# A hybrid attention, HGRN2 and MLP block: the means of query and key squares as two rounded passes, with GpSimd making remainders, and a reordered first stage

## The reference

```
u = rmsnorm(x);  proj = u @ w_in            # 1024 x 4096: q, k, v of attention, hq, two gates, hv, hg
y_na = neighbourhood attention, 8 heads of 64:
       q, k = rmsnorm over the 64 of each head (mean of squares, then rsqrt), times a weight
       scores on a window of 8 rows by 16 columns of a 16 x 64 grid, plus bias; softmax; times v
y_hg = HGRN2, 4 heads of 128, forward and backward, normed and gated
h = x + concat(y_na, y_hg) @ w_out
h = h + relu(rmsnorm(h) @ w_up)^2 @ w_down  # 4096 hidden
```

## Time and profile before

| | us |
|---|---|
| median of 3 runs | 1322.95 |
| profiled execution | 1322.97 |
| its span | 1321.0 |
| PE busy | 1289.5 (98%) |
| DVE busy | 868.1 (66%) |
| ACT busy | 583.6 (44%) |
| POOL busy | 478.3 (36%) |
| mean granted clock of PE | 0.996 |

### The profile page before, as it was taken

One profiled execution on the slowest core, in us unless ns is written; L12 is line 12 of the kernel. 1 busy time (PEld: TensorE's weight loads), 2 busy tenths in 40 slices (PEclk: granted clock), 3 DMA queues, 4 the chain that ended last, 5 costly groups with the idle time before them and its releaser, 6 DMA issues.

```text
span 1321.0 us, 17673 instructions
## 1 busy us (share of the span) xinstructions
PE 1289.5 (98%) x6432; PEld 1079.9 (82%) x6432; DVE 868.1 (66%) x1260; ACT 583.6 (44%) x1049; POOL 478.3 (36%) x259
## 2 busy tenths in 40 slices
PE   7999899999999999999999999999999999999998
PEld 5767787998888888887887788888888788888887
DVE  3456567551788795977468655455455898888885
ACT  5436566444344453333145645445544333432341
POOL 3251121123323132123423545545443454445452
PEclk9999899999999999999999999999999999999999
DMA  8341333232111011023420654444469563443433
GB/s 257 110 129 32 76 97 92 63 95 64 33 32 29 21 32 33 17 97 150 137 96 5 211 167 144 143 152 161 131 218 325 198 237 109 141 162 112 146 95 142
DMA packets 134324, 154.92 MB, mean 117 GB/s; under 512 B 11360, under 2 KB 89440, under 8 KB 134240
## 3 DMA queue, kind: packets, MB, share of 16 engines
q1 hardware_dynamic: 130032, 147.04, 34.6%
q10 hardware_dynamic: 4208, 6.76, 1.4%
HBM read 109.72 MB, written 44.04 MB: 116 GB/s over the span
## 4 chain that ended last, share of the span: by engine, by line
PE 84%; DVE 8%; ACT 3%; issue 2%; DMA 1%; POOL 1%; SPq 0%; ACTq 0%; DVEq 0%
PE bank L2288 8%; PE bank L2292 8%; PE bank L2291 8%; PE bank L2257 7%; PE bank L2260 7%; PE bank L2261 7%; PE bank L2003 5%; PE bank L2007 5%; PE bank L2006 5%; PE bank L2087 3%; PE bank L2214 2%; PE bank L2218 2%; PE bank L2217 2%; PE bank L1901 1%; PE bank L1990 1%
## 5 line engine op out<-in xcount | busy, mean ns | idle before, releaser
L927 POOL TENSOR_TENSOR a_split<-a_raw,a_split 128x1024 fp32r<-128x1024 f32 x56 | 148.0, 2658 | 166.1 <-ACT a_split L1200 166.1
L2257 PE MATMUL bank<-set,w_hi 128*128 128x512 f32 x448 | 177.8, 397 | 1.4 <-issue 1.1
L2260 PE MATMUL bank<-set,w_hi 128*128 128x512 f32 x448 | 176.2, 393 | 0.0
L2261 PE MATMUL bank<-set,w_lo 128*128 128x512 f32 x448 | 176.0, 393 | 0.0
L2288 PE MATMUL bank<-w_hi,a_split 128*128 128x512 f32 x448 | 174.6, 390 | 0.2
L2292 PE MATMUL bank<-w_hi,a_split 128*128 128x512 f32 x448 | 174.3, 389 | 0.0
L2291 PE MATMUL bank<-w_lo,a_split 128*128 128x512 f32 x448 | 174.3, 389 | 0.0
L2003 PE MATMUL bank<-uT_hi,w_hi 128*128 128x512 f32 x384 | 160.8, 419 | 2.5 <-DVE h_gate L1445 2.1
L2007 PE MATMUL bank<-uT_hi,w_lo 128*128 128x512 f32 x384 | 150.9, 393 | 0.0
L2006 PE MATMUL bank<-uT_lo,w_hi 128*128 128x512 f32 x384 | 150.3, 391 | 0.0
L874 POOL TENSOR_TENSOR w_hi<-stage,one_col 128x1024 fp32r<-128x1024 f32 x16 | 30.4, 1902 | 228.1 <-DVE bias L1489 95.9
(11 more groups left out here) (225 smaller groups left out, 2822.1 us busy)
## 6 DMA issues: line engine op xcount, KB each, us to landing
a_raw<-a_dram SPq DMA_DIRECT2D x56, 512.0 KB, 3.7
a_dram<-abuf SPq DMA_DIRECT2D x111, 256.0 KB, 2.1
stage<-in_w_in SPq DMA_DIRECT2D x29, 512.0 KB, 4.2
raw<-in_w_down SPq DMA_DIRECT2D x10, 1024.0 KB, 8.1
stage<-in_w_up SPq DMA_DIRECT2D x16, 512.0 KB, 5.2
raw_b<-in_w_up SPq DMA_DIRECT2D x16, 512.0 KB, 5.7
x_tok<-in_x SPq DMA_DIRECT2D x8, 512.0 KB, 9.9
v_dram<-vs ACTq DMA_DIRECT2D x16, 256.0 KB, 2.5
```

Source lines behind the costliest of these rows:

```text
L927: pool.tensor_tensor(split_of(m, 1), a_raw[:, m % 4, :, :], split_of(m, 0).bitcast(F32), ALU.subtract).then_inc(b_lo, 1)
L2257: first = pe.matmul(dst, w[0], u[0], start=k == 0 and p in (1, 5, 6, 7), stop=False, skip_group_check=True)
L2260: pe.matmul(dst, w[0], u[1], start=False, stop=False, skip_group_check=True)
L2261: ins = pe.matmul(dst, w[1], u[0], start=False, stop=k == 3, skip_group_check=True)
```

## The change

- The means: ACT, behind the square, writes a rounded copy of the squares into `sq_split` (which lies over the value store `vs`, so that the first copy waits for value stores); POOL subtracts it from the squares into the second half (`square_lo`); PE makes two passes of rounded matmuls with a rounded copy of the constant matrix (`mean_r`) instead of one full float32 matmul. `qk_average(n - 1)` comes after four k steps of unit n instead of two, for n = 9 to 12. In the steps its place is as before.
- The low squares stand in POOL's list between splits: squares 0 and 1 ahead of the split of tile 8, 2 and 3 ahead of 9, 4 and 5 ahead of 10, and so on, two by two. The splits of tiles 8 and 9 wait in addition for the low parts of units 9 and 11. The loop over later splits is written out, and the splits of tiles 22 to 24, 25 to 27 and 29 to 31 wait for the end of the levels of head 0, 1 and 2; tile 32 waits, as 33 did, for the last head's.
- First stage: SP loads the identity alone ahead of the second token tile, and that ahead of the first value weights; the norm weights go on SP's queue behind them, the rest of the tables behind the tokens. ACT and DVE normalise a pair of tokens ahead of the value units of the pair before. The arithmetic for the gates' bounds and the clearing of `q_tiles` are moved ahead of the last value units.
- Band 2 is loaded ahead of tile 13 instead of 14. The first `hv` unit is in step 9 instead of 10, and ACT takes it at the end of that step.
- In the MLP's start POOL waits for three of DVE's sums ahead of its fifth low part, and ACT takes set 8 ahead of the first result.

The diff, cut to its core:

```
-VALUE_UNITS = {10: (0, 1, 2), 11: (3, 4, 5), ...
-BANDS_BEFORE = {14: (2, 3, 4), 15: (5, 6), ...
+VALUE_UNITS = {9: (0,), 10: (1, 2), 11: (3, 4, 5), ...
+BANDS_BEFORE = {13: (2,), 14: (3, 4), 15: (5, 6), ...
...
             load_x(0)
+            sp.dma_start(ident, tables[:, 0:P]).then_inc(tab_load, 16)
+            load_x(1)
             load_v_weights(0)
-            sp.dma_start(tab[:, :], tables).then_inc(tab_load, 16)
-            load_x(1)
+            ... sp.dma_start(norm_w[:, 0, :], ...).then_inc(norm_load, 16)
...
+            def square_lo(i):
+                pool.wait_ge(qk_sq_hi, i + 1)
+                pool.tensor_tensor(sq_split[:, 1, :], qk_t[:, 0, :], sq_split[:, 0, :].bitcast(F32), ALU.subtract).then_inc(qk_sq_lo, 1)
+            squares = 0
             for n in range(RING, 4 * RING):
+                if n in (8, 9):
+                    upto = 2 * (n - 7)
+                else:
+                    upto = min(max(2 * n - 14, 0), 16)
+                while squares < upto:
+                    square_lo(squares)
+                    squares += 1
+                if n in (8, 9):
+                    pool.wait_ge(qk_ready, qk_count(FIRST_QK + 2 * (n - 8) + 1))
                 if 10 <= n < 16:
                     pool.wait_ge(bias_done, bias_ops(2 * n - 19))
                 split_one(n)
-            split_turns(4, N_IN // RING)
-            for n in range(N_IN, N_IN + RING):
-                if n == N_IN + 1:
+            for n in range(4 * RING, N_IN + RING):
+                if 22 <= n < 28:
+                    pool.wait_ge(lev_taken, HEAD_PARTS * ((n - 16) // HG_GROUP - 1))
+                elif 29 <= n < N_IN:
+                    pool.wait_ge(lev_taken, HEAD_PARTS * (HG_HEADS - 1))
+                elif n >= N_IN:
                     pool.wait_ge(lev_taken, HEAD_PARTS * HG_HEADS)
                 split_one(n)
...
-            pool.wait_ge(t13_sum, 8)
+            pool.wait_ge(t2_sum, 3)
             up_lo(4)
...
                 act.activation(qk_t[:, 0, :], bank[n % 2][:, :], ACT.Square).then_inc(qk_sq, 1)
+                act.wait_ge(qk_sq, n - FIRST_QK + 1)
+                if n == FIRST_QK:
+                    act.wait_ge(v_stored[0], 32 * 4)
+                act.activation(sq_split[:, 0, :], qk_t[:, 0, :], ACT.Copy).then_inc(qk_sq_hi, 1)
...
-                pe.wait_ge(qk_sq, n - FIRST_QK + 1)
+                pe.wait_ge(qk_sq_lo, n - FIRST_QK + 1)
...
-                pe.matmul(bank[7][:, :], head_mean, qk_t[:, 0, :], start=True, stop=True).then_inc(qk_mean, 1)
+                pe.matmul(bank[7][:, :], mean_r[:, :], sq_split[:, 0, :], start=True, stop=False)
+                pe.matmul(bank[7][:, :], mean_r[:, :], sq_split[:, 1, :], start=False, stop=True).then_inc(qk_mean, 1)
...
-                projection(n, range(2))
+                projection(n, range(4))
                 qk_average(n - 1)
-                projection(n, range(2, KT))
+                projection(n, range(4, KT))
```

More of the change, by code:

```diff
@@ L50 @@
 FBLK = 2
+HG_GROUP = 3
 OUT_BLOCKS = KT // FBLK
@@ L151 @@
 STEP_UNIT = {s: BEFORE + 1 + s for s in range(-2, 9)}
[L153 to L155 removed]
+VALUE_UNITS = {9: (0,), 10: (1, 2), 11: (3, 4, 5), 12: (6, 7, 8), 13: (9, 10, 11), 14: (12, 13), 15: (14, 15)}
+BANDS_BEFORE = {13: (2,), 14: (3, 4), 15: (5, 6), 16: (7, 8), 17: (9, 10, 11), 18: (12, 13, 14), 19: (15,)}
 FIRST_HEAD = list(range(UNIT[("ff", 0, 0)], UNIT[("hq", 0, 1)] + 1))
@@ L237, in hybrid_block @@
         vs = nc.alloc_sbuf_tensor_at("vs", [P, 2, 2, HALF], F32, offset=end_attention)
+        sq_split = nc.alloc_sbuf_tensor_at("sq_split", [P, 2, HALF], F32R, offset=end_attention)
+        mean_r = nc.alloc_sbuf_tensor_at("mean_r", [P, P], F32R, offset=end_attention + 8192)
         x_tok = nc.alloc_sbuf_tensor_at("x_tok", [P, TT, D], F32, offset=work)
@@ L421, in hybrid_block @@
         tab_load = sem("tab_load")
+        mean_load = sem("mean_load")
         norm_load = sem("norm_load")
@@ L443, in hybrid_block @@
         qk_sq = sem("qk_sq")
+        qk_sq_hi = sem("qk_sq_hi")
+        qk_sq_lo = sem("qk_sq_lo")
+        mean_ready = sem("mean_ready")
         qk_mean = sem("qk_mean")
@@ L684, in _ @@
             load_x(0)
+            sp.dma_start(ident, tables[:, 0:P]).then_inc(tab_load, 16)
+            load_x(1)
             load_v_weights(0)
-            sp.dma_start(tab[:, :], tables).then_inc(tab_load, 16)
-            load_x(1)
+            with nc.allow_non_contiguous_dma(reason="small parameter vector"):
+                sp.dma_start(norm_w[:, 0, :], attn_norm_w.rearrange("o (k p) -> p (o k)", p=P)).then_inc(norm_load, 16)
             load_v_weights(1)
@@ L695, in _ @@
                 load_x(t)
+            sp.dma_start(tab[:, P:3 * P], tables[:, P:3 * P]).then_inc(mean_load, 16)
             for n, (kind, where) in enumerate(TILES):
@@ L840, in _ @@
         def _(pool):
[L841 to L850, removed]
             pool.wait_ge(ready_cols, 2)
@@ L861, in _ @@
                 pool.tensor_tensor(v_weight(w_lo, k), v_raw_weight(k), hi.bitcast(F32), ALU.subtract).then_inc(w_split, 1)
[L863 to L868, removed]
             def split_one(n):
@@ L1203, in _ @@
             act.preload_act_table_set("natural_log_exp_and_others")
-            with nc.allow_non_contiguous_dma(reason="small parameter vector"):
-                act.dma_start(norm_w[:, 0, :], attn_norm_w.rearrange("o (k p) -> p (o k)", p=P)).then_inc(norm_load, 16)
             act.wait_ge(ready_cols, 2)
@@ L1218, in _, with rms_pair @@
             v_weights(7)
-            for g in range(1, T_PAIRS):
+            def rms_pair(g):
                 for t in (2 * g, 2 * g + 1):
@@ L1222, in _ @@
                     rms(0, t)
+            rms_pair(1)
+            for g in range(1, T_PAIRS):
                 for k in range(KT):
                     take_uT(g, k)
+                if g + 1 < T_PAIRS:
+                    rms_pair(g + 1)
                 unit(2 * g - 2)
                 unit(2 * g - 1)
+                if g == 2:
+                    act.wait_ge(lb_diff, 1)
+                    act.activation(lb[:, :, :], lb[:, :, :], ACT.Exp).then_inc(lb_exp, 1)
             for dst, a, b in ((na_mask[:, :, :, :].rearrange("p s r c -> p (s r c)"), M_NA, M_END),
@@ L1229, in _ @@
                 act.dma_start(dst.bitcast(I32), masks[:, a // 4:b // 4]).then_inc(mask_load, 16)
+            act.wait_ge(mean_load, 16)
+            act.activation(mean_r[:, :], head_mean, ACT.Copy).then_inc(mean_ready, 1)
             unit(TT - 2)
             unit(TT - 1)
-            act.wait_ge(lb_diff, 1)
-            act.activation(lb[:, :, :], lb[:, :, :], ACT.Exp).then_inc(lb_exp, 1)
             for n in range(FIRST_QK, BEFORE - 2):
@@ L1246, in _ @@
                 values = [UNIT[("hv", 0, 0)] + i for i in VALUE_UNITS.get(s, ())]
-                for n in values[:1]:
+                for n in values[:1] if s > 9 else ():
                     unit(n)
@@ L1250, in _ @@
                     take_pT(s, 2)
-                for n in values[1:2]:
+                for n in values[1:2] if s > 9 else ():
                     unit(n)
@@ L1266, in _ @@
                         score_exp(s + 2, g)
+                if s == 9:
+                    for n in values:
+                        unit(n)
                 if s >= 0:
@@ L1317, in _ @@
             up_weights(5)
+            take_set(8)
             take_c11(0)
-            for g in range(8, 16):
+            for g in range(9, 16):
                 take_set(g)
@@ L1622, in _ @@
             dve.memset(one_col[:, :], 1.0).then_inc(ready_cols, 1)
[L1623 to L1626, removed]
+            for t in range(4):
+                normalise_tokens(0, t)
+                if t == 1:
                     dve.wait_ge(norm_load, 16)
+                    for k in range(KT):
+                        take_uT(0, k)
+            for g in range(1, T_PAIRS):
                 for k in range(KT):
                     take_uT(g, k)
-                if g:
-                    value_lo(2 * g - 2)
-                    value_lo(2 * g - 1)
-            dve.wait_ge(uT_done, 16)
[L1634 to L1641, removed]
+                if g + 1 < T_PAIRS:
+                    normalise_tokens(0, 2 * g + 2)
+                    normalise_tokens(0, 2 * g + 3)
+                value_lo(2 * g - 2)
+                value_lo(2 * g - 1)
+                if g == 1:
+                    dve.wait_ge(c_load, CONSTS)
+                    dve.tensor_tensor(lb[:, :, :], lb_raw[:, :, 1, :], lb_raw[:, :, 0, :], ALU.subtract).then_inc(lb_diff, 1)
+            dve.wait_ge(uT_done, 16)
+            for i in range(2):
+                dve.memset(q_tiles[:, i, :, :, :, :].bitcast(F32), 0.0).then_inc(cleared, 1)
             dve.wait_ge(lb_exp, 1)
@@ L1648, in _ @@
             dve.wait_ge(params, 1)
+            value_lo(TT - 2)
+            value_lo(TT - 1)
+            dve.wait_ge(mask_load, 32)
             for n in range(FIRST_QK, BEFORE - 2):
```

(8 more changed lines are left out.)

2 lines of the change are left out of this document (1 added, 1 removed).

## The result

The changed kernel took 1324.48 us (median of 20 runs, 1321.89 to 1331.16), the kernel before 1322.13 in 20 runs on the same chips: ratio 1.0022 [1.0011, 1.0032], so slower by about 3 us. The forecast was 8.1 us slower: the sign was right and the time lay in the range, the size was wrong. The profiled execution took 1331.16 us with a span of 1329.3, more than any other of the 20: that it equals the forecast is chance. A second profile of the same kernel (experiment 1) took 1325.47 and stands nearer to the median.

What follows compares the result with a forecast made beforehand. TensorE, busy 1289.5 of 1321.0 us, was taken as the bound. Terms of -2.7, +20.4, +1.7, -6.8, -3.0 and -1.5 sum to +8.1 on 1322.95, so 1331 us, range 1316 to 1338.

Steps and rivals of the forecast that it cites:

- the clock behind the stands: TensorE's clock drops after its three stands before means 8, 10 and 12: 7.0 us lost (1.7, 2.8, 2.5).
- Later, -1.5: After step 9: gathered splits free VectorE, 0.5 us off h_gate waits; 1.0 us gained in the MLP's start.
- first stage: Kernel start: earlier token tile 1 (1.3 us) and no x_tok waits in third transposes (1.4 us), together 2.7 us gained.
- order on GpSimd: Means 8 to 14: low squares queue behind splits, so TensorE stands; 20.4 us lost, 13.4 queueing and 7.0 clock.
- steps 0 to 8: Attention steps: stalls of 0.4 us per mean eat the 0.41 saved per pass; 1.7 us lost.
- band: Band 2 loaded before tile 13: the 4.6 us wait and 2.8 of clock go; 6.8 us gained net.
- value unit: A value unit moved into step 9 fills idle TensorE time there: 3.0 us gained.
- The point named as deciding the sign: Gains of 14 us are spent when splits ahead of squares 2 and 4 cost TensorE more; each 5 to 6 standing.
- The queue does not bind: Rival: low squares come when copies are done, so the change is 20 us faster, 1303 us; chance 0.12.
- the stands cost no clock: Rival: TensorE's stands bring no clock drop, so the 7.0 us fall away, 1324 us; chance 0.12.
- VectorE is blocked in every step: Rival: GpSimd's subtractions delay VectorE's work by 1.3 us each, 8 us on top, 1339 us; chance 0.10.
- The likeliest case: The forecast itself: whole kernel at 1331 us, own range 1325 to 1336; chance 0.66.

Runs made afterwards that it cites:

- experiment 1: The changed kernel again, unchanged, for a second profile: 1324.43 us, ratio 1.0024 to the kernel before.
- experiment 5: Changed kernel without the new means (one fp32 pass, no ACT copy or GpSimd low part, issued after two k steps): 1304.9 us, ratio 0.9872 to before.
- 6: Changed kernel with the band loads as before (band 2 again ahead of tile 14): 1331.93 us, ratio 1.0077 to the kernel before.
- 7: Changed kernel with the value units as before (unit 0 again in step 10): 1327.1 us, ratio 1.004 to the kernel before.
- experiment 2: Changed kernel with low squares 0 to 4 ahead of splits 8 and 9 in GpSimd's queue: 1319.24 us, ratio 0.9983 to the kernel before.
- 10: Changed kernel, two rounded passes kept, low squares computed on VectorE instead of GpSimd: 1308.27 us, ratio 0.991 to the kernel before.
- experiment 4: Changed kernel with 22, 24 and 20 unused matmuls ahead of means 8, 10 and 12 to keep TensorE busy: 1321.55 us, ratio 1.0002 to before.
- experiment 9: Changed kernel with fp32 means, value remainders of units 6 and 7 ahead of the bound's arithmetic, tile 32 ungated: 1302.97 us, ratio 0.9859 to before.
- experiment 3: Changed kernel with tile 32 split without waiting for the last head's levels: 1324.0 us, ratio 1.0023 to the kernel before.
- 8: Changed kernel with low squares 0 to 4 ahead of split 8, 5 ahead of 9, 6 ahead of 10: 1322.07 us, ratio 1.0006 to before.

## Why the prediction was wrong in size

Two terms of the sum were mis-sized: the clock behind the stands (7.0, measured 4 to 5), and above all the term "Later, -1.5", which by what is left came to about -5. Term by term, in us; measured is a difference of two rows of the table above, good to 2 or 3; "first stage and later" is what several leave, good to 4.

| step | forecast | measured | by |
|---|---|---|---|
| means: order on GpSimd and steps 0 to 8 | +22.1 | +20.1 | 1 less 5 |
| band | -6.8 | -7.0 | 1 less 6 |
| value unit | -3.0 | -2.1 | 1 less 7 |
| first stage and later | -4.2 | -7.8 | the rest |
| sum | +8.1 | +3.2 | 1 |

- **The order on GpSimd: mechanism right.** Split 8 stands ahead of square 2 and 9 ahead of 4, with the distances forecast from mean 8 on (8.9, 12.3, 8.9, 10.0, then 21.8 for two) against 8.35, 12.2, 7.7, 10.0 and 21.7. Split 7 ahead of square 0 set mean 8 in experiment 1, but not in the first profile. That stand was 2.68 us for 3.9 forecast, since split 7 ended at 72.26, 3.5 us earlier than in the earlier trace rows, while PE came 2.4 earlier. The point named as deciding the sign held as well: experiment 2 takes away the two stands and ends below before. "The queue does not bind" (1303) is refuted by experiments 2, 5 and 10.
- **Its clock part: mis-sized.** 7.0 was sized as three drops like the one in the earlier trace rows. The clock fell that low, 0.50 to 0.56, but experiment 4 puts the worth at 4.3 to 5.0. By distances between means, experiment 1 against 4, the three drops cost 0.5, 1.7 and 2.3 us (forecast 1.7, 2.8, 2.5). The first costs little because mean 9 waits for its chain anyway: 0.45 us behind the drop, 1.38 at full clock. The second varies: mean 11 came 7.7 to 9.1 us behind mean 10 in the six profiles with this order, 6.2 at full clock, and 8.9 was forecast. The rival "the stands cost no clock" (1324) has the time measured, but by another way: the stands did cost clock.
- **"Later": the largest wrong step.** The first stage itself was right: mean 8 of experiment 9, without a wait, is at 69.60; before, it was at 73.20 with 1.24 of wait, so 2.4 were gained (forecast 2.7). Thus the surplus lies later. From mean 23 to the end the old span has 1094.8 us, that of experiment 1 1084.8 and that of experiment 9 1084.0; 3.1 of the 10.0 and 10.8 are the value unit now ahead of the mean. The 6.9 and 7.7 left stand against 4.5 forecast for that stretch (value unit and later). It is not the MLP: only 1.5 of the 10.8 lie behind the start of the output projection, for 1.0 forecast. Ahead of it 0.5 was forecast for `h_gate` and nothing for the other waits of the HGRN stage. There TensorE's waits for `h_gate`, `queries` and `scores` were 2.1, 0.8 and 0.6 us; in experiment 1 3.2 of these 3.5 are gone, in experiment 9, where tile 32 is ungated, 1.8. That is the step that failed; what is left of the surplus no wait names. VectorE's busy time over the span fell from 868.1 to 839.9 us (experiment 9) with the same 1260 instructions, and in 240 to 600 from 243.4 to 219.4 (experiment 5), as it would if the gathered splits no longer lie over it. That they are the cause was not tested by a run of its own.
- **Missed:** the stretched arithmetic of the bound ahead of mean 8 (a stand of 5.69 us in the first profile), and the load behind tile 32. That tile's gated split held SyncE's queue, `na_back` was issued at 588.50 in the first profile and TensorE stood 2.73 at 602.26; experiment 3 shows that it costs no more than the `h_gate` waits that it saves.
- **A misreading:** for step 9 the prediction has 1.6 us of clock; the earlier trace rows give 0.12 of 11.16 busy us, 1.3.
- **Steps 0 to 8** behaved as forecast: waits of 0.40 to 0.43 at each mean. "VectorE is blocked in every step" (1339) did not come true in the steps, but it is what experiments 2 and 8 met when the splits were moved there.

The likeliest case was right in mechanism with its own range of 1325 to 1336; the median lies 0.5 below it.

## What to carry to other kernels

Before work goes on an engine that runs long instructions in order, list what stands ahead of each new instruction: here means that need a subtraction of 1.3 us, put behind splits of 4.3, cost 20 us, and 15 less with the subtraction on another engine. A cheaper pass is worth only what the chain in front of it leaves: 6.6 us of saved passes were lost on GpSimd and on VectorE, and plain fp32 means won. Price edits one at a time: 17 us of good ones hid behind one bad one, and the whole looked like nothing. And look whether the profile that a theory is drawn from is a typical execution: that of experiment 5 was 7 us above its median.

## What the runs showed of the hardware

- Scalar instructions of 128x8 elements on VectorE took 1.2 to 2.2 us where one of GpSimd's 128x1024 splits was under way at their start, and 0.13 to 0.17 where none was. They ended with that split: L1672 in the first profile at 67.49, the split at 67.46. So the wait goes by GpSimd's instruction, not by the size of VectorE's. The reciprocal at 63.67 in experiment 1, beside a split from 63.56 to 65.46, took 0.20. The Trainium skill, SBUF — State Buffer, section "Who interferes with whom", says that a VectorE instruction in a mode that uses both of its ports and a GpSimd instruction exclude each other for the whole instruction, and that `tensor_scalar` can enter such a mode. L1672 and the scaling of probabilities (4.37 us for two) are scalar operations on one tensor, and the trace agrees.
- The clock behind a stand differed between executions of one kernel: 0.56 in 75 to 80 behind the first stand of 5.69 us, 0.79 there behind that of 2.68; behind the stand of 6.0 us ahead of mean 10 the next mean came after 7.7 to 9.1 us in six profiles and after 6.2 with matmuls put into the stand, which kept the clock at 1.00.
